# Four pieces of the first layer's modulation moved from VectorE to TensorE, and their loads moved behind the weights

## The chip, the cores and the metric

The kernel runs on one NeuronCore of a Trainium2 chip, as one program. The metric is the device time of one execution in microseconds (us). Engines are named as the profile names them: PE (TensorE matmuls), PEld (its weight loads), DVE (VectorE), ACT (ScalarE), POOL (GpSimd), SP (SyncE, which here only issues DMAs).

## The reference, cut to what matters

Two blocks of transformer layers run one after another on 256 tokens of width 1024. The change lies in the first layer of the first block:

```
c_act = silu(c)                                  # c: one row of 1024
ada = c_act @ ada_w[l] + ada_b[l]                # [6 * 1024]
sh1, sc1, g1, sh2, sc2, g2 = split(ada, 6)
h = x * (1 + sc1) + sh1
y = even_mixer(h, ...)                           # NSA attention (8 heads) and DSA attention (8 heads)
x = layer_norm(ALPHA * x + (1 + g1) * y)
h = x * (1 + sc2) + sh2                          # after the attention
y = square(relu(h @ mlp_w1)) @ mlp_w2
x = layer_norm(ALPHA * x + (1 + g2) * y)
```

`ada_w[0]` is taken in twelve pieces of 512 columns, numbered j = 0 to 11. Pieces 0 to 3 are sh1 and sc1 (needed first), 4 and 5 are g1 (needed when the attention's output is added), 6 to 9 are sh2 and sc2 (needed before the first MLP), 10 and 11 are g2. In NSA each head has two branches over all 256 tokens (selected and window) and a small compressed one; in DSA each query keeps its 64 best keys, which are found by repeated max-of-8 over an index score.

## The kernel before, in words

All engines run hand-ordered instruction streams; semaphores tie them together. `Signal.up` raises a counter that an instruction reaches, `.at(name)` is the value to wait for.

**Weights.** SP walks one list, `LOADS`. An item is a 1 MB chunk of weights (`w`), half of a modulation piece (`("ada", l, j, kc)`, 1 MB), or a raw matrix. Most items land in a ring of four slots (`SLOTS = 4`): item n of the ring waits until item n-4 has been consumed (`ring_free`). SP is in order, so an item whose slot is not free holds back all that follow. The items in `BY_SELF` do not use the ring: the ten halves of pieces 4 to 8 land in buffers that are idle in this stage (`o_high`, `o_low`, `x_tok`, `hT`), each waiting for the previous user of its buffer (`LAND_BEFORE`). Functions in `BESIDE` issue small or shared loads (bias table, second-stage matrices) just ahead of the item they are tied to. A weight chunk is split by ACT into a rounded high part (`round_weights`, L515; it waits for the landing and for the last use of the chunk that held the same one of two places) and by DVE into the rest (`lower_weights`, L521), after which its ring slot is free. PE multiplies three products of the parts (`split_mm`, L527 to L529).

**Modulation pieces.** There are two ways to make a piece. Pieces 0 to 3 go by PE: `ada_products` (L603) issues, for each half, four matmuls with a stationary 128x32 tile from `c_wide` (column 0 of each tile holds a part of c_act, the other 31 columns are zero) and 512 moving columns of the weights; each of the four writes its own 32 partitions of a PSUM bank. ACT copies the bank to `ada_acc` (`ada_parts`, L612). The other pieces go by DVE: `ada_op` does eight multiply-adds of 128x512 (L623 once, L626 seven times). Either way PE then sums over partitions (`ada_sum`, four 1-column matmuls, L644, or one product with a matrix of ones for gate rows, L641), and DVE adds the bias (`ada_put`, L658).

**Stages around the change.** Ahead of the attention, `ev_tensor` projects the inputs chunk by chunk (w0 to w5), with DVE's pieces 4 to 7 put between its other work (`ev_vector`). `attention_tensor` then has a loop d = 0 to 7 over pairs of NSA units: logits of units 2d and 2d+1, turn (transpose, L1149) of unit 2d-3, then a part that differs with d (d = 0: `project` of w6 and `turn_compressed`, L827; d = 1, 2: half of w7 each; d = 3 to 6: two small `ql` products), `two_values_tensor(d-2)`, and the turn of unit 2d-2. Then come the two logits of DSA, the output product with chunk `EV_OUT` (w8), and steps 2 to 11, each with up to one head's logits, one turn, one `values` product and one projection, with w9 at step 3; `out_tail` multiplies by w10 and w11. A unit passes DVE (logits plus bias and row minimum, L1125 and L1126), ACT (exp, L1134), DVE (coefficient, L1409 to L1414), POOL (scale, L1141), PE (turn), ACT (copy, L1156). DVE also does the 8 rounds of selection (L1395, L1400) in units 2 to 14, and in DSA two `ada_op` after each head's logits, 16 in all, for pieces 8 and 9.

**PSUM.** Eight banks are handed out in rotation by `Banks.take`, which waits until the bank's last content was read.

## Time and profile before

| | |
|---|---|
| median of 3 runs | 1134.73 us (1134.62 to 1137.34) |
| profiled execution, its own time | 1136.48 us |
| span of that profile, first to last instruction | 1134.7 us |
| mean granted TensorE clock | 0.979 |
| busy: PE, DVE, ACT, POOL | 1079.1, 750.5, 608.9, 91.5 us |
| layer 0: projections / NSA / DSA (about) | 36 to 99 / 99 to 138 / 138 to 180 us |
| first MLP starts (about) | 198.5 us |

The profile page gives totals; the stage views give one row for each stretch of time, with the busy time of each engine, the granted clock and the share of the 16 DMA engines. A PE stretch that is busy throughout may still contain short waits, because ends of matmuls are modelled. In a timeline row the bracket holds the idle time ahead of the row and what ended it.

### The profile page before, as it was taken

The numbers are of one execution on the slowest core, as the hardware profiler recorded it, in microseconds if no ns is written. First come the engines' busy times: TensorE is split into PE (matmuls) and PEld (weight loads), VectorE is DVE, ScalarE is ACT, GpSimd is POOL, SyncE is SP. The second block draws the span as 40 slices with busy tenths as digits, with TensorE's granted clock in tenths as the row PEclk, the third lists the DMA queues.
The fourth block names the chain that finished last, engine by engine and source line by source line (L and its number), as shares of the span: only waits on it lengthen the run. The fifth ranks groups of instructions, "written<-read, shape, count | busy, mean of one in ns | idle before, by whom it ended". The sixth has DMA issues, their size and how long they took to land.

```text
span 1134.7 us, 19834 instructions
## 1 busy us (share of the span) xinstructions
PE 1079.1 (95%) x8085; PEld 958.0 (84%) x8085; DVE 750.5 (66%) x1254; ACT 608.9 (54%) x1098; POOL 91.5 (8%) x120
## 2 busy tenths in 40 slices
PE   6999998999999999989999999999779999999998
PEld 3988576989899899978899988999668878999986
DVE  1686887898997866567846446777477756444443
ACT  2544755644444556656545464546765536555453
POOL 0002771000000000000000000031430000000000
PEclk8999999999999999999999999999689999999999
DMA  9998116699998455333865653250000145555541
GB/s 370 393 393 359 39 38 259 248 357 357 352 349 299 170 186 182 130 126 139 337 218 186 222 186 114 75 225 36 2 1 21 39 154 198 188 186 185 186 149 38
DMA packets 33562, 218.27 MB, mean 192 GB/s; under 512 B 4528, under 2 KB 5296, under 8 KB 8896
## 3 DMA queue, kind: packets, MB, share of 16 engines
q1 hardware_dynamic: 33472, 217.00, 51.6%
q8 instruction: 65, 1.06, 0.4%
q14 instruction: 25, 0.20, 0.1%
HBM read 215.93 MB, written 1.05 MB: 191 GB/s over the span
## 4 chain that ended last, share of the span: by engine, by line
PE 74%; DVE 10%; ACT 8%; DMA 4%; POOL 2%; issue 2%; DVEq 0%; SPq 0%; ACTq 0%; POOLq 0%
PE bank L527 20%; PE bank L529 19%; PE bank L528 19%; ACT high L515 2%; DVE low L521 2%; DMA ring<-ada_halves 2%; DMA ring<-chunks 1%; POOL zb L1141 1%; PE bank L567 1%; PE bank L2484 1%; PE bank L644 1%; DVE y_tmp L1607 1%; DVE stats L1609 1%; DMA o_land<-ada_halves 1%; DVE y_tmp L1596 1%
## 5 line engine op out<-in xcount | busy, mean ns | idle before, releaser
L521 DVE TENSOR_TENSOR low<-ring,high 128x2048 fp32r<-128x2048 f32 (+1 forms) x139 | 317.8, 2288 | 236.4 <-ACT high L515 236.1
L515 ACT ACTIVATE high<-ring 128x2048 fp32r<-128x2048 f32 (+1 forms) x139 | 264.7, 1906 | 246.4 <-PE bank L529 193.2
L527 PE MATMUL bank<-act_high,high 128*128 128x256 f32 (+1 forms) x1072 | 308.2, 288 | 0.0
L529 PE MATMUL bank<-act_high,low 128*128 128x256 f32 (+1 forms) x1072 | 303.6, 283 | 0.0
L528 PE MATMUL bank<-act_low,high 128*128 128x256 f32 (+1 forms) x1072 | 303.5, 283 | 0.0
L527 PE MATMUL bank<-high,act_high 128*128 128x512 f32 (+1 forms) x632 | 233.9, 370 | 3.1 <-DVE act_low L3079 1.8
L528 PE MATMUL bank<-low,act_high 128*128 128x512 f32 (+1 forms) x632 | 231.2, 366 | 0.0
L529 PE MATMUL bank<-high,act_low 128*128 128x512 f32 (+1 forms) x632 | 231.2, 366 | 0.0
L527 PEld LDWEIGHTS bank<-act_high,high 128*128 128x128 f32 x1072 | 204.7, 191 | 4.5 <-issue 2.1
L528 PEld LDWEIGHTS bank<-act_low,high 128*128 128x128 f32 x1072 | 204.9, 191 | 2.5 <-issue 1.4
L529 PEld LDWEIGHTS bank<-act_high,low 128*128 128x128 f32 x1072 | 204.8, 191 | 0.0
L527 PEld LDWEIGHTS bank<-high,act_high 128*128 128x128 f32 x632 | 119.4, 189 | 23.5 <-DVE act_low L3079 2.0
L529 PEld LDWEIGHTS bank<-high,act_low 128*128 128x128 f32 x632 | 119.4, 189 | 20.6
L528 PEld LDWEIGHTS bank<-low,act_high 128*128 128x128 f32 x632 | 119.6, 189 | 17.9
L626 DVE SCALAR_TENSOR_TENSOR ada_acc<-ring,c_act,ada_acc 128x512 f32<-128x512 f32 x105 | 79.4, 756 | 4.6
L1134 ACT ACTIVATE zb<-zb,ust 128x128 f32<-128x128 f32 x80 | 35.5, 446 | 26.6 <-DVE ust L1126 26.6
L2364 POOL MEMSET conv<- 128x24 f32 x1 | 0.1, 122 | 539.1 <-DVE x_tok L2122 539.1
L1141 POOL TENSOR_SCALAR zb<-zb,ust 128x128 f32<-128x128 f32 (+1 forms) x48 | 40.2, 852 | 32.0 <-DVE ada_cols L658 14.3
L582 PEld LDWEIGHTS bank<-cols 128*128 128x128 f32 x286 | 35.6, 203 | 5.1 <-issue 5.0
L582 PE MATMUL bank<-cols 128*128 128x128 f32 x286 | 37.6, 288 | 0.0
L1149 PE MATMUL bank<-cols,zb 128*128 128x128 f32 x96 | 16.9, 288 | 8.0 <-DVE zb L1954 2.5
L1149 PEld LDWEIGHTS bank<-cols,zb 128*128 128x128 f32 x96 | 10.8, 143 | 14.6 <-DVE zb L1954 2.7
(512 smaller groups left out, 1348.3 us busy)
## 6 DMA issues: line engine op xcount, KB each, us to landing
ring<-chunks SPq DMA_DIRECT2D x138, 1024.0 KB, 4.9
ring<-ada_halves SPq DMA_DIRECT2D x38, 1024.0 KB, 5.0
o_land<-ada_halves SPq DMA_DIRECT2D x6, 1024.0 KB, 11.5
ring<-raw_cmp SPq DMA_DIRECT2D x4, 1024.0 KB, 11.2
x_tok<-ada_halves SPq DMA_DIRECT2D x3, 1024.0 KB, 14.7
gate_rows<-ada_b SPq DMA_DIRECT2D x4, 512.0 KB, 9.3
bias<-bias_by_distance SPq DMA_DIRECT2D x1, 2048.0 KB, 13.1
ln_rows<-ln_g SPq DMA_DIRECT2D x4, 512.0 KB, 5.9
```

Of the source, the lines that this page charges most:

```text
L515: e.activation(weights(c)[0], in_ring(("w", c)), ACT.Copy).then_inc(*act.up("high", c))
L521: e.tensor_tensor(low, in_ring(("w", c)), high.bitcast(F32), ALU.subtract).then_inc(*vec.up("low", c))
L527: e.matmul(out_, ah, bh, start=start, stop=False)
L528: e.matmul(out_, ah, bl, start=False, stop=False)
L529: return e.matmul(out_, al, bh, start=False, stop=stop)
L567: last = e.matmul(out_, src[:, k, toks], w[:, k, c0:c0 + n_cols], start=k == 0, stop=k == n - 1)
L582: m = e.matmul(b[:, 0:P], ident, ident, start=True, stop=True)
L626: e.scalar_tensor_tensor(acc, w_[:, k, :], c_, acc, ALU.mult, ALU.add).then_inc(*vec.up("ada_op", l, j, i))
L644: m = e.matmul(b[:, i:i + 1], acc[:, i * P:(i + 1) * P], ones[:, 0:1], start=True, stop=True)
L1134: x = e.activation(z[:, c], z[:, c], ACT.Exp, bias=st[:, t:t + 1], scale=-1.0, accum_out=st[:, 2 + t:3 + t])
L1141: x = e.tensor_scalar(z[:, c], z[:, c], st[:, 4 + t:5 + t], None, ALU.mult)
L1149: m = e.transpose(b[:, tok(i)], z[:, tok(i)], ident)
```

## The change

The halves of pieces 6 to 9 go into the ring, behind w7 and before w8, instead of into borrowed buffers between w3 and w8. Only four halves (pieces 4 and 5) stay outside the ring. The products of pieces 6 to 9 are made by PE in iterations d = 1 to 4 of the NSA loop, copied by ACT in the same iteration, summed by PE at the end of iterations d = 2 to 5, and their bias is added by DVE at units 7, 9, 11 and 13. DVE's 32 `ada_op` of these pieces go. The stationary tiles need a second buffer, `c_late`, because `c_wide` shares memory with others by then; DVE fills it once, ahead of w6's low part. The bias table's load moves from ahead of piece 8 to ahead of w6, and three waits that pointed at DVE's pieces 7 and 8 point at piece 5.

```diff
+        c_late = mem.take("c_late", KT, 32, at=spare_at + 2 * NB * UC)
...
-            *raw_("cmp", 0, 0), *raw_("cmp", 0, 1), *raw_("cmp", 1, 0), ("ada", 0, 5, 1), *raw_("cmp", 1, 1), ("ada", 0, 6, 0),
-            *w(3), *raw_("ksv"), *raw_("vwg"), *w(4), ("ada", 0, 6, 1), ("ada", 0, 7, 0), *w(5), ("ada", 0, 7, 1), *w(6),
-            ("ada", 0, 8, 0), *w(7), ("ada", 0, 8, 1), *w(8), *ada(0, 9), *w(9, 10, 11),
+            *raw_("cmp", 0, 0), *raw_("cmp", 0, 1), *raw_("cmp", 1, 0), ("ada", 0, 5, 1), *raw_("cmp", 1, 1),
+            *w(3), *raw_("ksv"), *raw_("vwg"), *w(4, 5, 6, 7), *ada(0, 6), *ada(0, 7), *ada(0, 8), *ada(0, 9), *w(8, 9, 10, 11),
...
-        LAND_OF = ("o_high", "o_low", "x_tok", "o_high", "o_low", "x_tok", "o_high", "o_low", "x_tok", "hT")
+        LAND_OF = ("o_high", "o_low", "x_tok", "o_high")
...
-            return (pe if item[0] == "raw" or item[1] == 0 and item[2] < 4 else vec).at(*item)
+            return (pe if item[0] == "raw" or item[1:3] in ON_TENSOR else vec).at(*item)
...
+        ON_TENSOR = [(0, j) for j in (0, 1, 2, 3, 6, 7, 8, 9)]
...
+            c_ = c_wide if j < 4 else c_late
...
             project(e, 4, "q0")
-            ada_sum(e, 0, 6)
...
             ada_put(e, 0, 4)
-            ada_half(e, 0, 6, 0)
...
             lower_weights(e, 4)
-            ada_half(e, 0, 6, 1)
-            ada_half(e, 0, 7, 0)
             compress_vector(e)
...
-            ada_half(e, 0, 7, 1)
-            ada_put(e, 0, 6)
+            e.memset(c_late, 0.0).then_inc(*vec.up("c_late_zero"))
+            e.wait_ge(*vec.at("c_late_zero"))
+            e.tensor_copy(c_late[:, :, 0], c_act).then_inc(*vec.up("c_late"))
             lower_weights(e, 6)
...
                     turn_compressed(e)
-                    ada_sum(e, 0, 7)
...
                 if d >= 2:
                     two_values_tensor(e, d - 2)
+                if 1 <= d < 5:
+                    if d == 1:
+                        e.wait_ge(*vec.at("c_late"))
+                    ps.take(e, ("parts", 5 + d), act, "ada", 0, 5 + d, 1)
+                    for kc in range(2):
+                        ada_products(e, 5 + d, kc)
                 if d >= 1:
                     unit_turn_tensor(e, 2 * d - 2, pool)
+                if 2 <= d < 6:
+                    ada_sum(e, 0, 4 + d)
...
-                if step == 6:
-                    ada_sum(e, 0, 8)
...
-            ada_sum(e, 0, 9)
             e.wait_ge(*vec.at("o", "dsa", 7))
...
                 unit_logits_scalar(e, 2 * d + 1)
+                if 1 <= d < 5:
+                    ada_parts(e, 5 + d)
...
-                if u == 1:
-                    ada_put(e, 0, 7)
+                if u in (7, 9, 11, 13):
+                    ada_put(e, 0, 6 + (u - 7) // 2)
...
                 mask_bias(h + 2)
-                for _ in range(2):
-                    modulation_part()
...
-        BESIDE = {2: early_loads, 4: second_loads, LOAD_AT["ada", 0, 5, 0]: lambda e: gate_load(e, 0, 0), LOAD_AT["ada", 0, 6, 1]: compression_loads, LOAD_AT["ada", 0, 8, 0]: mixer_loads,
+        BESIDE = {2: early_loads, 4: second_loads, LOAD_AT["ada", 0, 5, 0]: lambda e: gate_load(e, 0, 0), LOAD_AT["w", 4]: compression_loads, LOAD_AT["w", 6]: mixer_loads,
```

## Rows read from the trace of the kernel before

**Rows 1.** The page: busy us, share of the span, instructions of each engine.
```profile
PE 1079.1 (95%) x8085; PEld 958.0 (84%) x8085; DVE 750.5 (66%) x1254; ACT 608.9 (54%) x1098; POOL 91.5 (8%) x120
```
**Rows 2.** Stretches: length, busy of each engine (instructions), clock, DMA share, GB/s.
```profile
112.30:118.40 6.10, 6.10 (x53) 4.75 (x52) 4.06 (x25) 3.20 (x12) 4.64 (x7) 1.00 0.01 3
121.60:125.45 3.85, 3.85 (x31) 2.13 (x30) 3.09 (x20) 3.17 (x13) 2.65 (x4) 1.00 0.00 0
129.08:134.20 5.12, 4.53 (x32) 2.33 (x31) 4.11 (x13) 4.32 (x13) 1.93 (x3) 1.00 0.10 19
134.20:138.26 4.06, 3.20 (x23) 1.88 (x23) 3.85 (x23) 3.61 (x14) 3.92 (x6) 1.00 0.64 242
158.17:160.48 2.31, 2.31 (x15) 1.65 (x13) 2.31 (x8) 0.61 (x2) 0.09 (x1) 1.00 0.00 0
168.18:172.40 4.22, 2.48 (x14) 1.75 (x13) 2.56 (x9) 1.91 (x7) 2.52 (x3) 1.00 0.13 54
172.60:176.00 3.40, 3.40 (x12) 2.24 (x12) 0.48 (x1) 2.56 (x3) 1.45 (x2) 0.50 0.87 325
```
**Rows 3.** Chain of waits, us 99 to 185: start, length, what.
```profile
107.34 0.79 PE bank L644 x8
...
123.74 0.28 DVE zb L1125
...
...
130.46 2.10 DVE low L521
...
165.60 0.52 PE bank L1149 x3
```
**Rows 4.** PE's timeline: start, length, instruction [idle before].
```profile
69.17 3.69 PE L561 MATMUL bank<-hT,ring 128*128 128x256 f32 x16 [0.96 <-ACT high L515]
...
106.71 0.63 PE L827 MATMUL bank<-cols,pc 128*128 128x128 f32 x4 [0.77 <-DVE pc L1058]
...
151.69 0.52 PE L1149 MATMUL bank<-cols,zb 128*128 128x128 f32 x3 [0.95 <-DVE dbias L1427]
...
162.78 0.52 PE L1149 MATMUL bank<-cols,zb 128*128 128x128 f32 x3 [1.38 <-POOL zb L1141]
...
172.43 0.73 PE L1149 MATMUL bank<-cols,zb 128*128 128x128 f32 x3 [1.78 <-DVE act_low L1166]
...
180.37 0.50 PE L527 MATMUL bank<-high,act_high 128*128 128x512 f32 x1
```
**Rows 5.** SP, ACT and DVE timelines around w7's landing.
```profile
83.47 0.33 SPq L3265 DMA_DIRECT2D ring<-chunks  x1
...
96.85 0.38 ACT L835 ACTIVATE qT<-bank 128x256 f32<-128x256 f32 x1 [2.49 <-PE bank L529]
98.83 1.92 ACT L515 ACTIVATE high<-ring 128x2048 fp32r<-128x2048 f32 x1 [1.60 <-DMA ring<-chunks]
...
102.99 0.47 DVE L1039 SCALAR_TENSOR_TENSOR pc<-bank,bc 128x120 f32<-128x120 f32 x2
```
**Rows 6.** PE's timeline, pieces 1 and 3, where products run already.
```profile
15.50 1.06 PE L603 MATMUL bank<-ring,c_wide 128*32 128x512 f32 x8 [0.25 <-DMA ring<-ada_halves]
...
29.85 1.93 PE L603 MATMUL bank<-ring,c_wide 128*32 128x512 f32 x16
```
**Rows 7.** Instructions of ada_acc: count, duration ns min/median/max, starts.
```profile
L612 ACT ACTIVATE ada_acc<-bank x4: 597/597/597, 10.9 to 31.8; 128x512 f32<-128x512 f32 x4
```
**Rows 8.** POOL's scaling pair, in NSA and in DSA beside DVE's pieces.
```profile
122.53 1.50 POOL L1141 TENSOR_SCALAR zb<-zb,ust 128x128 f32<-128x128 f32 x2 [0.17 <-DVE ust L1414]
...
170.16 2.13 POOL L1141 TENSOR_SCALAR zb<-zb,ust 128x128 f32<-128x128 f32 x2 [1.59 <-DVE ust L1409]
```
**Rows 9.** DVE's timeline, head 7 of DSA.
```profile
169.34 0.29 DVE L1125 CUSTOM_DVE_ANT_0 zb<-bank,dbias 128x128 f32<-128x128 f32 x1 [1.49 <-PE bank L1107]
...
169.98 1.52 DVE L626 SCALAR_TENSOR_TENSOR ada_acc<-ring,c_act,ada_acc 128x512 f32<-128x512 f32 x2
...
171.96 0.42 DVE L1166 TENSOR_TENSOR act_low<-bank,act_high 128x256 fp32r<-128x256 f32 x1 [0.46 <-ACT act_high L1162]
```

More of the change, by code:

```diff
@@ L460, in program @@
         o_lands = [mem.take(f"o_land{i}", KT, SEQ, at=split_at[i] + KT * L2) for i in range(2)]
-        LANDS = {"o_high": o_lands[0], "o_low": o_lands[1], "x_tok": x_tok, "hT": hT}
-        LAND_OF = ("o_high", "o_low", "x_tok", "o_high", "o_low", "x_tok", "o_high", "o_low", "x_tok", "hT")
+        LANDS = {"o_high": o_lands[0], "o_low": o_lands[1], "x_tok": x_tok}
+        LAND_OF = ("o_high", "o_low", "x_tok", "o_high")
         BY_SELF = {("ada", 0, 4 + i // 2, i % 2): (name, LAND_OF[:i].count(name) + 1) for i, name in enumerate(LAND_OF)}
@@ L596, in program @@
         ADA_N = {a: n for n, a in enumerate(ADA_ORDER)}
+        ON_TENSOR = [(0, j) for j in (0, 1, 2, 3, 6, 7, 8, 9)]
         def ada_products(e, j, kc):
             w_, b = in_ring(("ada", 0, j, kc)), ps.of(("parts", j))
+            c_ = c_wide if j < 4 else c_late
             e.wait_ge(*ring_landed(("ada", 0, j, kc)))
             for k in range(4):
-                m = e.matmul(b[32 * k:32 * k + 32, :], c_wide[:, 4 * kc + k, :], w_[:, k, :], start=kc == 0, stop=kc == 1)
+                m = e.matmul(b[32 * k:32 * k + 32, :], c_[:, 4 * kc + k, :], w_[:, k, :], start=kc == 0, stop=kc == 1)
             m.then_inc(*pe.up("ada", 0, j, kc))
@@ L638, in ada_sum @@
             b = ps.take(e, ("ada", n), vec, "ada_put", n)
-            e.wait_ge(*(act if l == 0 and j < 4 else vec).at("ada", l, j, 1))
+            e.wait_ge(*(act if (l, j) in ON_TENSOR else vec).at("ada", l, j, 1))
             if j // 2 in (2, 5):
@@ L1160, in head_out_scalar @@
             if stage == "nsa" and i == 0:
-                e.wait_ge(*vec.at("ada", 0, 7, 1))
+                e.wait_ge(*vec.at("ada", 0, 5, 1))
             e.activation(oH[:, i, :], ps.of(name)[:, 0:SEQ], ACT.Copy).then_inc(*act.up("o_high", stage, i))
@@ L1415, in coefficient @@
                     *vec.up("coef", u))
-            parts = iter([(j, i) for j in range(8, 10) for i in range(8)])
-            def modulation_part():
-                j, i = next(parts)
-                ada_op(e, 0, j, i)
             def mask_bias(h):
@@ L1479, in attention_vector @@
                 mask_bias(step + 2)
-                if step < 8:
-                    for _ in range(2):
-                        modulation_part()
-                if step == 6:
-                    ada_put(e, 0, 8)
                 if step in (3, 8):
@@ L1489, in attention_vector @@
                     head_out_vector(e, 4 + h // 2, ("heads", 4 + h // 2), "dsa")
-            ada_put(e, 0, 9)
             lower_weights(e, MLP0)
@@ L3209, in residual_load @@
         def residual_load(e):
-            e.wait_ge(*vec.at("ada", 0, 8, 0))
+            e.wait_ge(*vec.at("ada", 0, 5, 0))
             for t in range(QT):
@@ L3253, in sync @@
                 if item in BY_SELF:
-                    if item == ("ada", 0, 8, 1):
-                        e.wait_ge(*pe.at("raw", "vwg"))
                     for before in LAND_BEFORE[item]:
```

## The prediction

> **What bounds the kernel now.** I read the page first: PE is busy 95% of the span [rows 1], so whatever adds PE work must be paid back by PE's own waits. Then the stretch view, cut at the loop steps of the attention [rows 2], to see where PE has waits at all; then the chain of waits from 99 to 185 us [rows 3], to see who sets the pace; then PE's timeline for each wait and its releaser [rows 4]. The reader is to see three regions. Up to iteration d = 4 of NSA (about 123.7 us) PE works without gaps: the 6.10 and 3.85 us stretches are busy throughout. From there to about 165.6 us the chain runs through DVE, ACT and POOL, and PE has gaps [rows 2, 3]. In DSA one head's step of 2.31 us at full PE pace becomes 4.22 us later on, and from 172.6 to 176.0 us the granted clock is 0.50, the 1.2 GHz level of the two (1.2 and 2.4), after a wait of 1.78 us [rows 2, 4]. From the first MLP on PE is the bound again, and nothing of the change lies there.
>
> **Part 1, ahead of d = 1: PE saves 3.3 us.** Pieces 6 and 7 no longer stand in the load order between w3 and w7. (a) The wait of 0.96 us at 69.17 us is for a raw matrix's landing behind half 6.0, although the row names ACT's last signal [rows 4]; half a piece less ahead of it is 1 MB, and the wait goes: -0.96. (b) The sums of pieces 6 and 7 leave this region, 0.79 us each [rows 3]: -1.6. (c) w7 was issued at 83.47 us and landed at 98.83 us [rows 5]; with no piece around it and the bias ahead of w6 it should land before 90 us. What that is worth is small: w7's rounding also waits for w5's last use, which ends with q1's copy at 96.85 us [rows 5]. It moves from 98.83 to about 97.2 us in the old time, less another 1.8 us from (a) and (b's first sum). So DVE's `pc` chain, 102.99 to 106.57 us, comes 3.4 us earlier, and PE's wait of 0.77 us for it at 106.71 us goes [rows 4, 5]: -0.77. Together -0.96 - 1.58 - 0.77 = -3.3. DVE's 16 multiply-adds of pieces 6 and 7 (7 x 0.75 + 0.48 = 5.7 us a piece) are otherwise worth nothing here, since PE works from 69.17 us on with 1.2 us of other waits. The new fill of `c_late` is two small DVE instructions, under 0.5 us, in a stretch where DVE waits for ACT: 0.
>
> **Part 2, NSA d = 1 to 7: PE pays 10.1 us.** The products run already for pieces 0 to 3. At the full clock a half (8 records) takes 0.95 to 1.06 us, and a whole piece 1.93 us [rows 6]. Four pieces: +7.7 us. PE has no gap in d = 1 to 4 [rows 2], so I cost them in full. Four sums of 0.79 us now end d = 2 to 5: +3.2; the last is in d = 5, where the chain has left PE, so I take 0.8 off. 7.7 + 3.2 - 0.8 = +10.1. From d = 5 on DVE sets the pace (w8's low part at 130.46 us, then units 12 to 15 without a gap), and it starts from d = 5's logits, so the whole shift passes through to 138.26 us. ACT's four copies of 0.60 us [rows 7] lie in iterations that grow by 1.9 to 2.7 us and in which it was busy 3.17 of 3.85 us [rows 2]: 0. If that cover were gone they would cost up to 2.4. What queues behind PE's new waits: the turn of unit 2d-2 and all logits after it. The halves' landing is the one to watch. A ring slot for 8.0 is free when 6.0 has been multiplied in d = 1, for w8 when 8.0 has in d = 3. I put d = 1's products at 108.4 to 110.3 us, d = 3's at 122 to 124 us: 12 us between issue and use, against 15.3 us under a full queue (w7) [rows 5], but here the queue is nearly idle (DMA share 0.01) [rows 2], so it is hidden. Bounds of this part: below +5 (the part in d = 3 to 5, 6.3 us, mostly falls beside DVE), above +12.5 (ACT's copies on the path).
>
> On the price of the products a rule speaks against the change. At 15.50 us a half, four matmuls of 512 fp32 columns, takes 1.06 us [rows 6]. The Trainium skill, "FP8 and Floating Point Precision", TensorE Precision Notes, says that true FP32 takes four passes through the array; by that, as an estimate, 32 matmuls one after another at 2.4 GHz would be 32 x 4 x 512 / 2400 = 27.3 us. The row disagrees with that sum. The skill's "TensorEngine Tiling (Array Packing)", When to Use Tiling, has a 32-wide stationary operand as four-fold column tiling, which is nearer to the row. The sum here goes by the row.
>
> **Part 3, DSA: the kernel wins back 6.1 us.** Here 16 of DVE's multiply-adds go from between the heads' logits, with the sum of piece 8 (0.79 us, on PE's path; the sum of piece 9, just ahead of 180.37 us, lay beside the wait for the last head and is worth 0). Head 7 shows the mechanism: logits on DVE at 169.34 us, the pair of multiply-adds 169.98 to 171.50 us in front of the next DVE work, and POOL's scaling pair at 170.16 us taking 2.13 us, where alone it takes 1.50 us [rows 8, 9]. (The same 0.6 us is in the Trainium skill as a rule: "SBUF — State Buffer", Who interferes with whom, has a DVE instruction with two SBUF inputs contend with a GpSimd instruction that reads SBUF. By that rule POOL's pair goes to 1.50 us without the pieces.) I rebuild the steps: a turn can start when DVE logits of the following head (0.65 us), coefficient (0.16), POOL (1.50) and hand-overs (about 0.6) are done, 2.9 us after PE's logits; PE's own work between is 2.3 us, and a step of PE is 2.31 us [rows 2]. Steps 4 to 7 then take 4 x 2.31 + 0.2 + 0.85 (the last step has no logits to fill in) = 10.3 us, where they took 172.43 - 158.17 = 14.26: -4.0 with the sum in it. The 0.95 us at 151.69 us is POOL behind the same pair of engines: -0.95 [rows 4]. From the turn at 172.43 us to `out_tail` at 180.37 us are 8.0 us, 3.4 of them at half clock [rows 2, 4]; at the full clock these would be 1.7, but ACT's rounding of w11 (1.9 us) stands in that stretch, so I take -1.2. Sum -6.1. Bounds: -2.6 (only 0.79 + 0.95 and half of the two long waits' remainder at 162.78 us and 172.43 us) and -8.
>
> **The sum.** -3.3 + 10.1 - 6.1 = +0.7 us. Made against the profiled execution: its own time is 1136.48 us, its span 1134.7; the median of the runs is 1134.73, so +0.7 on that is **1135.4 us**. 0.3% of it is 3.4 us, about what a measurement of this kernel can tell from no change.
>
> **The rivals.**
> *Faster: the products fall into NSA's other waits.* The chain leaves PE at 123.74 us for DVE [rows 3], and in d = 6 and 7 PE is busy only 4.53 of 5.12 and 3.20 of 4.06 us [rows 2]. If DVE, ACT and POOL, given longer iterations, run ahead and need less time from d = 5 on, some 5 us of the 10.1 are absorbed: 1134.7 + 0.7 - 5 = 1130.4 us. For it: the chain. Against it: w8's rounding and low part stand in a fixed order on ACT and DVE whatever PE does. It decides from 4.1 us absorbed.
> *Slower: DSA's stalls stay.* If the waits at 162.78 and 172.43 us come from the order PE, DVE, ACT, DVE, POOL, PE itself, and not from the multiply-adds, only the sum, the 0.95 us and about 1 us return: -3.3 + 10.1 - 2.7 = +4.1, that is 1138.8 us. For it: the 1.78 us wait ends just as the output copy at 171.96 us does, which waits for ACT and not for a multiply-add [rows 4, 9]. It decides when part 3 gives less than 3.4 us. The half clock is part of it: if PE still waits near 172 us, it may fall again.
> *Slower by far: the products run one after another* as the four-pass rule has it: 27.3 - 7.7 = +19.6 on the sum, 1155 us. The rows at 15.50 and 29.85 us speak against it [rows 6]; I leave it 1 in 50.
> *The change doesn't do what it says:* w7 was not the bound because w5's last use was. That is in the sum already (part 1c); if even the 0.77 us stays, the result is 1136.2, within.
>
> **How the numbers follow.** Likeliest, break-even within 0.3%: 0.50, its own range 1132 to 1138. Absorbed in NSA: 0.24. DSA's stalls stay or NSA pays its upper bound: 0.24. One after another: 0.02. Range for 8 in 10: from the faster rival, 1130.0, to slightly past the slower one, 1140.5. Faster by over 0.3% 0.24, within 0.50, slower 0.26.
>
> **What the new profile would show.** Part 1: no PE wait at 69 us, w7 landed before 90 us and its rounding right behind q1's copy near 95.5 us, d = 1's logits near 104.8 us (were 108.06). Part 2: L603 rows of 1.9 us in each of d = 1 to 4, no DMA wait ahead of them, iterations of d = 2 and 3 longer by 2.7 us, DSA's first logits near 145 us. Part 3: POOL's pair at 1.5 us, steps of 2.3 to 2.9 us, no stretch at half clock, `out_tail` near 181 us (was 180.37). The prediction is wrong if DSA's first logits come before 142 us, if DSA's stretch shrinks by less than 3.4 us, or if PE waits for a half's landing.

## The result and the profile after

The changed kernel takes 1142.40 us (median of 11 runs, 1135.53 to 1147.61) where the kernel before, run between them on the same chip, takes 1135.73 (11 runs, 1134.62 to 1139.35): ratio 1.005, 95% interval 1.0034 to 1.0066. It is slower. The forecast was 1135.4, within 0.3%.

First the page of the changed kernel, its busy row:

```profile
PE 1092.6 (95%) x8149; PEld 964.8 (84%) x8149; DVE 728.4 (64%) x1224; ACT 609.3 (53%) x1102; POOL 86.1 (8%) x120
```

64 PE records more than in [rows 1] (the trace has two for each of the 32 new fp32 matmuls), and 22 us less of DVE. Now its stretches. The first seven stand for the same instructions as those of [rows 2]: d = 2, d = 4, d = 6 and d = 7 of NSA, then DSA's step 4, its step 7 up to the turn, and the way from that turn to `out_tail`, of which [rows 2] have the 3.4 us at half clock. The last two lie in the second block. Columns as in [rows 2].

```profile
110.53:119.23 8.70, 8.70 (x75) 6.08 (x74) 4.02 (x24) 4.16 (x15) 3.00 (x4) 1.00 0.67 252
125.13:132.29 7.16, 6.53 (x55) 3.51 (x54) 3.32 (x20) 4.12 (x15) 2.98 (x4) 1.00 0.86 320
137.28:142.54 5.26, 3.96 (x31) 2.12 (x30) 5.14 (x21) 4.42 (x18) 1.99 (x4) 1.00 0.45 146
142.54:145.71 3.17, 3.16 (x23) 1.89 (x24) 2.04 (x11) 1.79 (x7) 2.15 (x4) 1.00 0.25 103
165.15:167.46 2.31, 2.31 (x16) 1.65 (x14) 1.18 (x7) 0.96 (x4) 0.43 (x1) 1.00 0.46 103
172.78:176.41 3.63, 2.67 (x14) 1.70 (x14) 0.72 (x5) 2.87 (x11) 2.60 (x4) 1.00 0.00 0
176.41:183.46 7.05, 5.47 (x27) 3.34 (x27) 3.55 (x5) 5.11 (x10) 1.50 (x2) 1.00 0.15 24
860.00:870.00 10.00, 10.00 (x183) 8.29 (x180) 6.80 (x22) 4.39 (x13) 0.00 (x0) 0.87 0.01 3
870.00:880.00 10.00, 10.00 (x88) 7.97 (x87) 4.71 (x13) 2.05 (x6) 0.00 (x0) 0.50 0.17 54
```

PE's timeline of the changed kernel, with the idle time in the bracket:

```profile
67.92 2.40 PE L561 MATMUL bank<-hT,ring 128*128 128x256 f32 x10 [1.28 <-DMA ring<-raw_ksv]
...
103.75 0.60 PE L829 MATMUL bank<-cols,pc 128*128 128x128 f32 x4
104.28 0.49 PE L1114 MATMUL bank<-k_win,qT 64*128 64x128 f32 x4
...
108.20 1.92 PE L606 MATMUL bank<-ring,c_late 128*32 128x512 f32 x16
...
118.35 0.95 PE L647 MATMUL bank<-ones,ada_acc 128*128 128x1 f32 x8
119.23 0.49 PE L1114 MATMUL bank<-k_win,qT 64*128 64x128 f32 x4
...
136.29 1.05 PE L647 MATMUL bank<-ones,ada_acc 128*128 128x1 f32 x8 [0.67 <-DVE ada_cols L661]
...
142.54 0.49 PE L1114 MATMUL bank<-k_win,qT 64*128 64x128 f32 x4 [0.97 <-DVE ada_cols L661]
...
145.71 0.39 PE L1106 MATMUL bank<-ckvT,qlatT 128*128 128x128 f32 x2
...
176.41 0.52 PE L1149 MATMUL bank<-cols,zb 128*128 128x128 f32 x3 [0.63 <-POOL zb L1141]
...
178.80 0.52 PE L1149 MATMUL bank<-cols,zb 128*128 128x128 f32 x3 [0.64 <-POOL zb L1141]
183.46 0.50 PE L527 MATMUL bank<-high,act_high 128*128 128x512 f32 x1 [0.93 <-DVE act_low L1166]
```

Where the time went is read from the same instructions in both timelines. From raw `kv`'s first product (at 33.78 us here, at 35.34 before; before's profile had lost time at a reduced clock ahead of it, 0.58 from 25 to 30 us, so ends alone would mislead) to d = 1's logits it is 104.28 - 33.78 = 70.5 us, before 108.06 - 35.34 = 72.7: **-2.2**. From there to DSA's first logits 145.71 - 104.28 = 41.4, before 138.26 - 108.06 = 30.2: **+11.2**. From there to `out_tail` 183.46 - 145.71 = 37.75, before 180.37 - 138.26 = 42.11: **-4.4** [rows 2, 4]. From `out_tail` to the first MLP 18.1 in both. Sum +4.6 us. The trace of the changed kernel's second measurement (`after_again`, below) has the same three stretches within 0.4 us.

The profiled execution took 1147.61 us, 11.1 more than that of before. Some 8 us of this come after the first MLP, where the two programs are the same: both executions lose clock between 800 and 840 us, but at 870 us this one ran at 0.50 of the clock, and before's did not:

```profile
870.00:880.00 10.00, 10.00 (x178) 8.82 (x175) 5.60 (x16) 6.09 (x20) 0.00 (x0) 1.00 0.03 11
```

Such losses come and go from run to run: the mean granted clock of the kernel before went from 0.972 to 0.986. So beside each ratio below stands a second figure, **the difference to before at one clock**: over the 312 undisturbed executions of the 20 kernels whose clock is on record (125 of them of the kernel before, beside the experiments), device time is fitted as a constant of each kernel minus 0.744 us for each 0.001 of mean granted clock (what is left scatters by 0.97 us), and the constants are compared, with a 95% interval. By it the change costs +5.2 +- 0.6 us. The figure has a limit: where a kernel itself makes the clock fall, it takes that loss out too, so it prices the work and the waits and not the whole. A few executions that the chip disturbed as a whole are left out.

### The profile page after: what moved, and what is told of

It is laid out like the page before. It is cut to its first block, busy times and chain, and to the rows that moved or that the text cites. A ratio compares the mean times of both kernels' runs of the same rounds, so it can differ in the third digit from the quotient of the medians.

```text
span 1145.8 us, 19936 instructions
## 1 busy us (share of the span) xinstructions
PE 1092.6 (95%) x8149; PEld 964.8 (84%) x8149; DVE 728.4 (64%) x1224; ACT 609.3 (53%) x1102; POOL 86.1 (8%) x120
## 4 chain that ended last, share of the span: by engine, by line
PE 78%; DVE 8%; ACT 7%; DMA 3%; POOL 2%; issue 1%; SPq 0%; DVEq 0%; ACTq 0%; POOLq 0%
PE bank L527 21%; PE bank L529 20%; PE bank L528 20%; DMA ring<-ada_halves 2%; ACT high L515 1%; DVE low L521 1%; PE bank L567 1%; PE bank L2476 1%; POOL zb L1141 1%; PE bank L606 1%; PE bank L647 1%; ACT zb L1134 1%; DVE y_tmp L1599 1%; PE bank L2464 1%; DVE stats L1601 1%
## 5 line engine op out<-in xcount | busy, mean ns | idle before, releaser
L629 DVE SCALAR_TENSOR_TENSOR ada_acc<-ring,c_act,ada_acc 128x512 f32<-128x512 f32 x98 | 73.7, 752 | 4.4
L1141 POOL TENSOR_SCALAR zb<-zb,ust 128x128 f32<-128x128 f32 (+1 forms) x48 | 36.2, 768 | 50.6 <-DVE ust L1420 42.6
L582 PE MATMUL bank<-cols 128*128 128x128 f32 x286 | 35.2, 277 | 0.0
L1156 ACT ACTIVATE pT<-bank 128x384 f32<-128x384 f32 x32 | 15.3, 481 | 14.9 <-PE bank L1149 14.9
```

The source lines that it names most:

```text
L582: m = e.matmul(b[:, 0:P], ident, ident, start=True, stop=True)
L629: e.scalar_tensor_tensor(acc, w_[:, k, :], c_, acc, ALU.mult, ALU.add).then_inc(*vec.up("ada_op", l, j, i))
L1141: x = e.tensor_scalar(z[:, c], z[:, c], st[:, 4 + t:5 + t], None, ALU.mult)
L1156: e.activation(pT_of(u), ps.of(("turn", u))[:, 0:UC], ACT.Copy).then_inc(*act.up("pT", u))
```

## The experiments

**The change again, and a known cost.** `after_again` is the changed kernel once more. `shift12` is the kernel before with 12 idle products (0.23 us each, 2.8 us) put in front of the first MLP's second step; it asks whether later work or a later start of the second block costs more than its own length.

```diff
+                    if tag == "m0" and step == 1:
+                        idle_products(e, b, 12)
```

> The changed kernel once more, beside the kernel before on one chip, for the spread. If its mean clock (0.9785 in 11 runs, 0.9799 before) is worse because of the change, the median stays near 1142.4; if the clock's falls in the second block come and go by themselves, the median is 1140 to 1141, 5.3 us over the kernel before, as at equal clock.

> The kernel before, with 12 idle 128x128 products put into the first MLP's second step, where TensorE is never idle. Nothing else differs, so everything from there on runs 12 x 0.23 = 2.8 us later, about the 2.6 us by which the changed kernel is late there. Theory S (the changed kernel's loss beyond 3 us is the granted clock: the second block's stretch from 740 to 880 us falls to half clock at places that depend on when it runs): the time rises by more than 2.8 us or spreads over several us from run to run, median 1137 to 1142. Rival C (the change itself, by its order of PSUM banks or ring slots, slows the later stages): 2.8 us and no more, 1138.5 with the narrow spread of the kernel before.

`after_again`: 1138.59 us, ratio 1.0038 (1.002 to 1.0056), at one clock +5.1 +- 0.6. Its median lies 3.8 us under the first one's, with the mean clock at 0.9813 in place of 0.9785: the median of 11 runs depends on the draw of clocks, the figure at one clock does not. `shift12`: 1137.54, ratio 1.0023 (1.0008 to 1.0038), at one clock +2.8 +- 0.6. Work in PE's path costs its own length, and the adjustment finds 2.8 for 2.8. A later start of the second block costs nothing besides.

**Part 3: what DVE's pieces in DSA cost.** `thin_dsa` is the kernel before with the multiply-adds of pieces 8 and 9 cut to 16 of 512 columns (it leaves the values of these pieces out).

```diff
+            thin = slice(0, 16 if (l, j) in THIN else 512)
-                e.scalar_tensor_tensor(acc, w_[:, k, :], c_, acc, ALU.mult, ALU.add)
+                e.scalar_tensor_tensor(acc[:, thin], w_[:, k, thin], c_, acc[:, thin], ALU.mult, ALU.add)
```

> The kernel before, with VectorE's 16 multiply-adds of pieces 8 and 9 cut to 16 of 512 columns (their values are left out); loads, waits and sums stay. Prices part 3 alone. Theory of the prediction: the waits of DSA come from these instructions; the stretch from DSA's first logits to the output tail (42.1 us) shrinks by 5 us. Rival (the chain through VectorE, ScalarE, VectorE, GpSimd and TensorE itself sets the pace): by 3.6 us or less, as in the changed kernel (4.4 with the sum of 0.8).

1132.27 us, ratio 0.9971 (0.9958 to 0.9985), at one clock -2.9 +- 0.6, and -3.3 in DSA's stretch of its trace. That is a little over half of the 5.3 us that the prediction's part 3 had without the sum of piece 8. POOL's pair takes 1.5 us at every head of its trace, where beside DVE's full pieces it took 2.1 to 2.2. Its timeline still has waits in DSA's end, for POOL now:

```profile
168.09 0.52 PE L1152 MATMUL bank<-cols,zb 128*128 128x128 f32 x3 [1.15 <-POOL zb L1144]
170.48 0.52 PE L1152 MATMUL bank<-cols,zb 128*128 128x128 f32 x3 [0.64 <-POOL zb L1144]
```

`piece8_nsa` moves piece 8's eight multiply-adds to NSA's units 2 to 5 and spreads piece 9's; all is computed (on top of `w7_first`, below).

```diff
+                if 2 <= u < 6:
+                    for _ in range(2):
+                        modulation_part()
...
-                    for _ in range(2):
-                        modulation_part()
+                    modulation_part()
```

> The kernel before, with w7 loaded ahead of piece 8 as in w7_first, and VectorE's eight multiply-adds of piece 8 moved from DSA into units 2 to 5 of NSA, where VectorE waits for TensorE; one multiply-add per head stays in DSA. If DSA's waits come from the multiply-adds (16 of them cost 3.3 us in thin_dsa), half of them gone gives 1.6 us; NSA should not grow, since VectorE waits 0.4 to 2.0 us per unit there. Expected 1132.5 to 1134. Rival: units 4 to 6 do two rounds of selection each and VectorE is late for the logits from iteration 4 on: no gain.

1135.44 us, ratio 1.0001 (0.9987 to 1.0015), at one clock +0.2 +- 0.6. DSA's first logits to the last projection take 37.6 us (40.8 before), but NSA is 2.6 us longer: what DSA wins, NSA pays. `parts_last` and `parts_last_w7` ask whether the order inside a step is the cost: the two multiply-adds go behind the step's output copy.

```diff
-                if step < 8:
-                    for _ in range(2):
-                        modulation_part()
                 if step in (3, 8):
...
                     head_out_vector(e, 4 + h // 2, ("heads", 4 + h // 2), "dsa")
+                if step < 8:
+                    for _ in range(2):
+                        modulation_part()
```

> The kernel before, with VectorE's two multiply-adds of a step of the sparse attention moved behind that step's output copy (the low part of a pair of heads) and behind the low part of the weights; nothing else changes, and all is computed. If the stalls come from the output copy standing behind the multiply-adds, the wait of 1.78 us at 172.43 us shrinks to under 0.6 us and the time is 1 to 1.5 us under before: 1133.8 us at an equal clock. If they come from the 24 us of multiply-adds and POOL's slowed pair, nothing changes, 1135 us; the multiply-adds may also delay the next head's logits: 1136 us.

> parts_last with weight piece 7 loaded ahead of the half of piece 8 (w7_first). If both gains are real and add up, 1.5 to 2 us under before, 1133.3 us, ratio 0.998 to 0.999; if neither is, 1135 us.

1139.98 (ratio 1.0042, 1.0026 to 1.0057; at one clock +3.1 +- 0.8) and 1139.98 (1.0042, 1.0018 to 1.0067; +3.4 +- 0.6). The order matters, but the other way: the multiply-adds now stand between the output copy and the next head's logits, and PE waits longer: the stretch from DSA's first logits to `out_tail` is 45.6 us in its trace, before 42.1. The timeline of `parts_last`:

```profile
161.58 0.49 PE L1106 MATMUL bank<-ckvT,qlatT 128*128 128x128 f32 x2 [1.15 <-DVE ust L1126]
164.09 0.87 PE L1149 MATMUL bank<-cols,zb 128*128 128x128 f32 x3 [1.58 <-POOL zb L1141]
...
179.08 0.52 PE L1149 MATMUL bank<-cols,zb 128*128 128x128 f32 x3 [2.09 <-POOL zb L1141]
```

**Part 1: what leaves the region ahead of d = 1.** `thin_early` is the kernel before with DVE's work on pieces 6 and 7 cut as in `thin_dsa` (`THIN = [(0, 6), (0, 7)]`; their values are left out). `w7_first` changes one place of the load order (the bias table's load goes along). `ksv_first` is the changed kernel, `both_first` is `w7_first`, each with one more.

```diff
-            ("ada", 0, 8, 0), *w(7), ("ada", 0, 8, 1), *w(8),
+            *w(7), ("ada", 0, 8, 0), ("ada", 0, 8, 1), *w(8),
...
-            *w(3), *raw_("ksv"), *raw_("vwg"),
+            *raw_("ksv"), *w(3), *raw_("vwg"),
```

> The kernel before with VectorE's 16 products of pieces 6 and 7 cut to 16 of 512 columns; it leaves out the values of pieces 6 and 7. It does what part 1 of the change does for VectorE, with loads, sums and all else as before. If VectorE's work ahead of the attention holds TensorE only at the products of the compressed weights (0.77 us) and of the half of them at the sums, the time is 0.8 to 1.2 us under before, 1134.5 us. Rival, as the prediction had it: also the wait at 69.17 us falls (piece 6's half is released earlier), 1.7 to 2 us under before, 1133.5 us. Third: nothing, since the next wait behind VectorE takes the gain.

> The kernel before, with only the load of w7 (and the bias table's place) ahead of the first half of piece 8. w7 lands 2.5 us earlier, its rounding begins right after q1's copy near 97.2 us and the compressed softmax 1.6 us earlier. If part 1's account is right, TensorE's wait of 0.77 us at 106.71 us goes and the attention's later part, which VectorE paces, starts up to 1.6 us earlier: 0.8 to 1.6 us off the start of the first MLP. Rival (w7's landing was hidden): no change there.

> The changed kernel with the raw key weights ksv loaded one place earlier, ahead of weight piece 3. Theory: TensorE's wait of 1.28 us at 67.92 is set by the transfer of piece 3 that lies ahead of ksv behind a ring slot that comes free at 59.2 us, not by the modulation piece that the change took away; with the order turned ksv lands about a piece's transfer earlier (1 us or more) and the wait falls below 0.4 us, so the kernel is 0.9 to 1.3 us faster than the changed one: 1138.9 us at an equal clock. Rival: ksv's own slot or its own transfer sets the landing, the wait stays above 0.9 us and the time is the changed kernel's, 1140 us.

> The kernel before with weight piece 7 loaded ahead of the half of piece 8 (as in w7_first) and ksv ahead of weight piece 3. If both waits of TensorE (0.96 us at 69.17, 0.77 us and more at 106.71) go and come back nowhere, the time is 1.5 to 2.0 us under before, 1133.7 us, ratio 0.9985. Rival: the ksv wait moves to piece 3's product or to the raw v weights behind it, and the time is that of w7_first, ratio 0.9995 to 1.0005.

| | median us | ratio (95%) | at one clock |
|---|---|---|---|
| `thin_early` | 1135.77 | 1.0009 (0.9994 to 1.0025) | +0.6 +- 0.8 |
| `w7_first` | 1136.82 | 1.0004 (0.9986 to 1.0022) | -0.6 +- 0.6 |
| `ksv_first` | 1144.72 | 1.0095 (1.0077 to 1.0113) | +6.1 +- 0.8 |
| `both_first` | 1135.61 | 1.0006 (0.999 to 1.0022) | -0.2 +- 0.8 |

`thin_early` leaves the wait for the compressed weights where it was; w7's rounding still waits 1.60 us for w7's landing, as in [rows 5]:

```profile
104.25 0.63 PE L830 MATMUL bank<-cols,pc 128*128 128x128 f32 x4 [0.77 <-DVE pc L1061]
```

`w7_first` has no such wait, but `both_first`, with w7 in the same place, kept 0.65 us of it, and among the kernels with before's load order it is 0.77 us (before, `thin_early`), 0.38 (`empty_takes`), 0.21 (`shift12`) and none (`thin_dsa`). So it varies from one execution to the next with w7's landing, and one trace each doesn't show what the order is worth. The wait at the raw keys varies too, from none (`thin_all`) over 0.55 (`empty_takes`) to 1.28 us; the two kernels with ksv first have none. Neither is a gain that can be measured: `ksv_first` shows a wait of 1.21 us for ACT ahead of the compressed logits, where the changed kernel had 0.47:

```profile
94.82 1.96 PE L819 MATMUL bank<-kcT,qT 64*128 64x15 f32 x32 [1.21 <-ACT qT L837]
```

**Part 2: what NSA pays for.** Five edits of the changed kernel. `thin_products` cuts the products of pieces 6 to 9 to 32 of 512 columns, `thin_all` cuts their sums to one matmul in place of four as well (both leave out these values). `puts_early` puts DVE's `ada_put` one unit earlier, `turn_first` puts the products behind the turn of unit 2d-2, `late_sums` keeps the four pieces in the idle `hT` and sums and puts them in steps 4 to 7 of DSA (all is computed).

```diff
-                m = e.matmul(b[32 * k:32 * k + 32, :], c_[:, 4 * kc + k, :], w_[:, k, :], start=kc == 0, stop=kc == 1)
+                wide = slice(0, 512 if j < 4 else 32)
+                m = e.matmul(b[32 * k:32 * k + 32, wide], c_[:, 4 * kc + k, :], w_[:, k, wide], start=kc == 0, stop=kc == 1)
...
+                if l == 0 and 6 <= j < 10:
+                    m = e.matmul(b[:, 0:4], acc[:, 0:P], ones[:, 0:4], start=True, stop=True)
...
-                if u in (7, 9, 11, 13):
+                if u in (6, 8, 10, 12):
...
-                if 2 <= d < 6:
-                    ada_sum(e, 0, 4 + d)
...
+                if 4 <= step < 8:
+                    ada_sum(e, 0, 2 + step)
```

> The changed kernel with the products of pieces 6 to 9 cut to 32 of 512 moving columns (the other values are left out); waits, ScalarE's copies, sums and loads stay. Prices the products. The prediction charged 7.7 us (four times 1.93) in full. Theory (TensorE paces NSA in the changed kernel, so all of it counts): 6.5 to 7.5 us off, 1133 to 1134 us. Rival (VectorE and ScalarE pace it from iteration 4 or 5 on): 4 us or less off.

> The changed kernel with TensorE's products of pieces 6 to 9 cut to 32 of 512 columns (as in thin_products) and each of their four sums cut from four matmuls to one; it leaves out the values of pieces 6 to 9. It asks what parts 1 and 3 of the change are worth without part 2. My theory now (the gains were forecast too large: behind the copies ahead of the compression 0.5 us where 1.75 stood in the sum, in the sparse attention 4.4 us where 6.1 stood): at an equal clock the changed kernel lies 5.2 us above before; less products 4 x 1.5 us and sums 4 x 0.66 us, plus some 1.4 us of waits for VectorE's reading of the sums' bank that come up when the products no longer hide them: 5.2 - 6.0 - 2.6 + 1.4 = -2.0 us, so 1133.5 us, 1132.5 to 1135. The rival is the prediction's own sum (gains 3.3 and 6.1, what is left of products and sums 2.3): -7 us, 1128.5 us.

> The changed kernel, with the four bias additions of pieces 6 to 9 on VectorE at units 6, 8, 10, 12 in place of 7, 9, 11, 13. Theory bank (the new sums rotate through the same PSUM banks seven takes later, so the sum in iteration 5 and the logits of iteration 7 wait 0.67 and 0.97 us for VectorE's late bias addition): both waits go, DSA's first logits come 0.7 to 1.6 us earlier than at 145.71 us. Rival (VectorE's pace from iteration 5 on sets that point whatever TensorE does): the waits move to other rows, under 0.3 us.

> The changed kernel with one thing moved: in iterations 1 to 4 the products of a piece stand behind the turn of unit 2d-2, not ahead of it. Theory order (the products hold back the turn, ScalarE's copy of it and so ScalarE's exp of the second unit, which stands behind that copy, then VectorE and the rounding of w8): DSA's first logits come 1 to 2 us earlier, the time falls by as much. Rival (only the 7.7 us of products count, wherever they stand in the iteration): no change, within 0.5 us at DSA's first logits.

> The changed kernel with the four sums and puts moved out of the compressed and window attention into steps 4 to 7 of the sparse attention (the four pieces wait in the feature buffer, which is idle there). It computes all that the reference does. The sums are 3.5 us of TensorE, four bank takes and about 2.6 us of waits of the stretch; in the sparse attention some of the 3.5 us fall into its stalls. By this the time is 3 to 4 us under the changed kernel, 1136.7 us, still not under before. Rival: all of the sums' time is only moved and the waits return elsewhere: 1139.5 us.

| | median us | ratio (95%) | at one clock |
|---|---|---|---|
| `thin_products` | 1139.52 | 1.0035 (1.0012 to 1.0057) | +0.5 +- 0.6 |
| `thin_all` | 1134.94 | 1.0001 (0.9987 to 1.0014) | -0.8 +- 0.8 |
| `puts_early` | 1140.31 | 1.0056 (1.0035 to 1.0077) | +5.0 +- 0.8 |
| `turn_first` | 1143.25 | 1.0068 (1.0048 to 1.0088) | +6.1 +- 0.6 |
| `late_sums` | 1141.33 | 1.0055 (1.0029 to 1.0081) | +5.8 +- 0.6 |

Thin products take 4 x (1.86 - 0.33) = 6.1 us off PE's path, and the time at one clock falls by 4.7; thin sums take 2.7 more off, and it falls by 1.3 more. The rest comes back as waits, which stand in NSA of `thin_all`:

```profile
119.12 0.55 PE L1153 MATMUL bank<-cols,zb 128*128 128x128 f32 x3 [0.75 <-DVE ada_cols L665]
...
122.43 0.70 PE L1289 MATMUL bank<-dqT,ukT 64*128 64x256 f32 x4 [1.31 <-DVE act_low L1170]
...
127.87 0.70 PE L1289 MATMUL bank<-dqT,ukT 64*128 64x256 f32 x4 [0.57 <-ACT ada_acc L616]
...
133.49 0.65 PE L1253 MATMUL bank<-pcT,v_cmp 15*64 15x256 f32 x4 [1.25 <-DVE act_low L1170]
...
136.39 0.80 PE L1118 MATMUL bank<-k_win,qT 64*128 64x128 f32 x4 [0.97 <-DVE ada_cols L665]
```

All five stand at a `take`: a bank whose last reader has not run. The order of takes in the kernel names the same readers: the turn of unit 4 gets the bank of piece 6's sum, one `ql` product of d = 4 that of the first pair of heads, one of d = 5 that of piece 9's products, the third pair of heads that of the second, and the logits of unit 14 that of piece 9's sum. By the same order the two waits for `ada_cols` in the changed kernel, at 136.29 and 142.54 us, are for the sums of pieces 8 and 9. After these waits the clock of `thin_all` fell to the lower level too; the stretch from 134 to 142 us:

```profile
134.00:142.00 8.00, 7.03 (x37) 4.53 (x36) 5.72 (x32) 4.29 (x17) 5.58 (x8) 0.63 0.38 134
```

`thin_products` does the same (0.78 and 0.53 in the two 5 us stretches from 130 us), and its 12 runs have the lower mean clock, 0.9756 against 0.9800 in before's 125. That is why its median is 4 us above before and its figure at one clock is not: at 0.744 us for 0.001 the clock makes up 3.3 us. Whether the kernel or the draw of clocks is to blame is open.

With `puts_early` the waits for `ada_cols` are gone and others have their place, so NSA is no shorter (41.8 us from d = 1's logits to DSA's, 41.4 in the changed kernel; `turn_first` is judged by its runs alone):

```profile
128.41 0.70 PE L1285 MATMUL bank<-dqT,ukT 64*128 64x256 f32 x4 [0.64 <-ACT pT L1156]
140.90 0.65 PE L1249 MATMUL bank<-pcT,v_cmp 15*64 15x256 f32 x4 [1.28 <-DVE act_low L1166]
```

`late_sums` has its first DSA logits 2.6 us earlier than the changed kernel and its last projection at the same time (182.1 us both): four sums moved, nothing won. My forecast of 3 to 4 us for it was wrong.

**The banks by themselves, and parts 1 and 3 by themselves.** `empty_takes` is the kernel before with the changed kernel's eight `ps.take` in NSA, released where its copies and puts would stand, and no work. `takes_copies` adds four ACT copies of 128x512 to it. `no_part2` is the changed kernel without products, banks, copies, sums and puts; one matmul of 16 columns for each half frees its ring slot (the values of pieces 6 to 9 are left out).

```diff
+                if 1 <= d < 5:
+                    ps.take(e, ("parts", 5 + d), act, "e", 2 * d + 1)
                 if d >= 1:
                     unit_turn_tensor(e, 2 * d - 2, pool)
+                if 2 <= d < 6:
+                    ps.take(e, ("held", d), vec, "z", 2 * d + 3)
```

```diff
-                    ps.take(e, ("parts", 5 + d), act, "ada", 0, 5 + d, 1)
-                    for kc in range(2):
-                        ada_products(e, 5 + d, kc)
...
-                    ada_sum(e, 0, 4 + d)
+                    pe.also("ada_sum", ADA_N[0, 4 + d])
```

> The kernel before, in which the attention's program on TensorE takes eight further banks where the changed kernel takes them, and releases them where ScalarE's and VectorE's instructions ahead of the copies and puts end; no work is added. Bank theory: the rotation of eight turns over 8.5 instead of 6.5 times in a step, so TensorE waits for younger work: 2 to 3 us slower, 1137.5 us. Rival: the waits seen are only where slack shows, no cost: 1135 us.

> As empty_takes, with ScalarE copying 128x512 values four times where the changed kernel copies the products (0.58 us each, 2.3 us in all; from SBUF, into the buffer that is idle there), and the four banks released by these copies. If ScalarE's copies are the cost, 2 us or more above empty_takes; if the banks are, within 0.7 us of it.

> The changed kernel without part 2: no products, bank, copy, sum or put for pieces 6 to 9 (of each half one matmul of 16 columns is left, to free its ring slot; the values of pieces 6 to 9 are left out). It measures what parts 1 and 3 are worth together. The prediction's gains, 3.3 + 6.1 = 9.4, less the four halves' small matmuls (0.5): 1126 us. By the milestones of the changed kernel, 0.5 + 1.7 + 4.4 = 6.6 less 0.5, so 1129 us. If the gains were mostly never there (as thin_early, at no gain, says of part 1), 3.3 as thin_dsa, 1131.7 us.

| | median us | ratio (95%) | at one clock |
|---|---|---|---|
| `empty_takes` | 1137.79 | 1.0012 (0.9996 to 1.0027) | +1.8 +- 0.6 |
| `takes_copies` | 1140.69 | 1.0042 (1.0025 to 1.0059) | +3.5 +- 0.6 |
| `no_part2` | 1132.33 | 0.9974 (0.9959 to 0.999) | -3.8 +- 0.6 |

Eight banks that nobody fills cost 1.8 us at one clock (the ratio alone doesn't tell it from none). Its trace has 33.2 us from d = 1's logits to DSA's, before 30.2. The two longest waits there, which before doesn't have:

```profile
122.58 0.70 PE L1286 MATMUL bank<-dqT,ukT 64*128 64x256 f32 x4 [0.94 <-DVE act_low L1166]
...
132.44 0.65 PE L1249 MATMUL bank<-pcT,v_cmp 15*64 15x256 f32 x4 [1.37 <-DVE act_low L1166]
```

Before had 8 banks for about 6.5 takes in an iteration (two units, two turns, two `ql`, half a pair of heads); with two more it has 8 for 8.5, so each take waits for younger work. The copies add 1.7 us more, between the two forecasts (2 us or more if ScalarE's copies are the cost, under 0.7 if the banks are); the banks are also released later by them, and the run can't part the two. `no_part2` gives 3.8 us where its forecasts were 3.3, 6.1 and 8.9, the last by the prediction's gains. In its trace DSA's stretch is 4.1 us shorter than before's, as in the changed kernel, and NSA's 3.1 us longer. Its timeline has 0.9 us for the small matmuls and a wait that the full products had hidden, since the half's transfer is now late:

```profile
123.90 0.23 PE L1153 MATMUL bank<-ring,c_late 128*32 128x16 f32 x2 [1.48 <-DMA ring<-ada_halves]
...
130.30 0.70 PE L1293 MATMUL bank<-dqT,ukT 64*128 64x256 f32 x4 [1.09 <-ACT qlatT L1361]
```

## Why the prediction was wrong

It summed -3.3 + 10.1 - 6.1 = +0.7. The stretches of the changed kernel gave -2.2 + 11.2 - 4.4 = +4.6, and the runs +5.2 +- 0.6 at one clock. Each term missed to the same side. Of the gap of 4.5 us to the runs, 2.8 are gains that were too large, in parts 1 and 3, and 1.1 the price of part 2; the last 0.6 is of the size of the interval. None of the three signs that the prediction named for being wrong came: DSA's first logits stand at 145.71 us (not before 142), DSA's stretch shrank by 4.4 us (not less than 3.4), and PE waited for no half's landing. They watched each part for a large miss; this was three small ones.

*Part 1 (a), the wait at 69.17 us: wrong in its cause.* It did not go; it is 1.28 us, and 0.92 in `after_again`, about the 0.96 of before. The half 6.0 did not hold ksv back. SP's queue of the changed kernel and its stretch 55 to 60 us, then the same of the kernel before:

```profile
59.24 0.33 SPq L3255 DMA_DIRECT2D ring<-chunks  x1
60.10 0.33 SPq L3255 DMA_DIRECT2D ring<-raw_ksv  x1
...
55.00:60.00 5.00, 5.00 (x58) 3.54 (x60) 4.08 (x6) 0.38 (x1) 0.00 (x0) 1.00 0.51 211
```

```profile
60.80 0.33 SPq L3265 DMA_DIRECT2D ring<-chunks  x1
61.66 0.33 SPq L3265 DMA_DIRECT2D ring<-raw_ksv  x1
...
55.00:60.00 5.00, 5.00 (x43) 4.15 (x45) 4.72 (x8) 0.77 (x2) 0.00 (x0) 1.00 1.01 423
```

w3 is issued 59.24 - 33.78 = 25.5 us after raw `kv`'s first product, before it was 60.80 - 35.34 = 25.5: the ring slot sets it, when PE has read a raw matrix. From ksv's issue to its first product it is 67.92 - 60.10 = 7.8 us, before, with the half on its way, 69.17 - 61.66 = 7.5. The half had used DMA engines that without it are half idle (share 0.51 from 55 to 60 us, with it 1.01). I had asked what lay ahead in the list, and not what released the issue. `ksv_first` shows the other half of the lesson: with the wait removed, 0.7 us came back as a longer wait for ACT (1.21 us where 0.47 was), and its time is no better (+6.1 +- 0.8 against +5.2 +- 0.6 at one clock).

*Part 1 (b) and (c): right in the trace.* From the raw keys to the compressed logits, where the sum of piece 6 had stood, it is 27.3 us, before 28.1. w7's rounding starts behind q1's copy (95.09 us; forecast near 95.5), the 0.77 us wait is gone and d = 1's logits start at 104.28 (forecast near 104.8). From the compressed logits on the stretch is 9.03 us where it was 10.78, -1.75 against -1.56 forecast. `thin_early` (+0.6 +- 0.8) shows no gain from DVE's work there, as forecast. The 0.77 us were in part luck of the profile that the forecast was read from, since `thin_dsa` with before's load order has no such wait; the time of `w7_first` lies at -1.2 to 0 us.

*Part 2: the mechanism right, two terms mis-sized.* Products: 4 x 1.86 = 7.4 (forecast 7.7); by the row at 108.20 us a piece, eight matmuls of 512 columns in sixteen records, takes 1.92 us. The sum by the four-pass rule that the prediction set beside its own (the Trainium skill, "FP8 and Floating Point Precision", TensorE Precision Notes) would be, as an estimate, 27.3 / 4 = 6.8 us for it if they ran one after another. They did not: each record lasts 0.59 us and a new one starts every 0.12 us on average. Four groups side by side would need a quarter of that estimate, 1.7 us, so the trace is against running one after another and not against four passes. Sums: 4 x 0.88 = 3.5 (forecast 3.2), all four on PE's path. The 0.8 us that I took off because DVE sets the pace at the end never came: from d = 4 on the waits of PE sum to 2.6 us (0.64, 0.67, 0.34, 0.97), before to 1.8 (0.34, 0.36, 0.23, 0.86). What I had not counted is the PSUM rotation. The copies stood at "0" because the products were to cover them; without products `takes_copies` has them at 1.7 us (forecast for that case: up to 2.4). Shown is that banks and copies cost 3.5 us without products, and that 8.8 us of thinned products and sums return only 6.0 at one clock. How much of the 11.2 us each of them has with the products in place can't be told apart, since they hide behind each other.

*Part 3: the mechanism right, the size 1.7 us too large.* POOL's pair is at 1.5 us, as in NSA, and nothing runs at half clock; that DVE's two-input work had slowed it ([rows 8]: 2.13 us) is confirmed by `thin_dsa`, where only that work was cut short and the pair takes 1.5 us, and with it the rule of the Trainium skill in "SBUF — State Buffer", Who interferes with whom, which gives no size for this pair. POOL's timeline of the changed kernel:

```profile
169.44 1.51 POOL L1141 TENSOR_SCALAR zb<-zb,ust 128x128 f32<-128x128 f32 x2 [0.20 <-DVE ust L1415]
```

But the rebuilt step was wrong. I had let each head go at PE's 2.31 us; heads 4 to 7 took from 165.15 to 176.41 = 11.3 us (forecast 10.3, before 14.26), since the round PE, DVE, ACT, DVE, POOL, PE is longer than PE's own work between, and 0.3 to 0.9 us of wait stay at five places. The 0.95 us at 151.69 gave 0.5 in its stretch. The 1.2 us in front of `out_tail` gave 7.94 - 7.05 = 0.9: the half clock and the sum of piece 9 went, and a new wait of 0.93 us for the last output copy came. The half clock doesn't belong to before's instructions alone: `w7_first` has the same wait of 1.78 us and kept the full clock from 169 to 175 us, with 40.9 us for DSA's stretch in place of 42.1. `thin_dsa` prices DVE's pieces alone at 2.9 +- 0.6 us. The rival "DSA's stalls stay" had 2.7 for the whole of part 3, the sum 6.1; 4.4 lies between. Its time, 1138.8 us, is near the 1140.3 us that the changed kernel has at a mean clock of 0.981 (before: 1135.0), but by luck in part: it counted the whole 3.3 us of part 1, where 2.2 came, and 2.7 us for part 3, where 4.4 came.

*The chances.* "Likeliest, break-even" rested on three errors that had to cancel; they had one sign, because each gain was read as the full length of a wait and each cost as the bare length of an instruction, in part 2 with 0.8 us off.

## What to carry to other kernels

Where engines hand work round in a ring, take a wait seen in a trace as an upper bound of what its removal gives, and look at a second trace of the same kernel to see whether the wait is always there. Here 9.4 us were counted as gain, 2.4 of them three sums that PE no longer makes there; 6.6 us were found in the stretches, and with the load order alone no gain could be measured. Before you move work onto an engine, count what it takes besides time: here two more bank takes in an iteration that had 6.5 for 8 banks. And where transfers wait for slots, ask what frees the slot before you credit a shorter list.

## What the runs showed of the hardware that was not expected

The same program's time varies by 11 us from run to run on one core at a time (before: 1131.6 to 1142.8 us in 125 runs, on four chips), and most of that goes with the mean granted clock at 0.744 us for each 0.001, much of it as stretches at the 1.2 GHz level in the second block. Kernels with PE work taken out of NSA fell to that level there, after the waits shown above: `thin_all` ran at 0.50 from 136 to 142 us, `thin_products` at 0.53 from 135 to 140 us, where before and the changed kernel kept 2.4 GHz. So a part of what the cut gave was taken back as clock in these executions. The same wait doesn't always bring it: PE waited 0.47 us ahead of the compressed logits in both the changed kernel and `puts_early`; the one kept 1.00 behind it, the other had 0.80 and 0.85 in the next two stretches of 5 us.

The products of a piece overlap on PE: sixteen records of 0.59 us each, on four groups of 32 partitions, take 1.92 us together.
